# Attention output written by columns: values stationary, turned probabilities moving, reciprocal sums spread by TensorE

## What is computed

```python
# first stack, units 0 and 1: window attention with a sink; units 2 and 3: neighbourhood attention
o = jnp.einsum("bnhgqk,bnkhd->bnqhgd", p.astype(v.dtype), vw)     # window_gqa
o = jnp.einsum("brhqik,brikhd->brqhd", p, vg)                     # neighborhood_attn
y_c = window_gqa(...) * jax.nn.silu(c_z)
y_d = neighborhood_attn(...) * jax.nn.silu(d_z)
...
x + jnp.einsum("bse,ed->bsd", y, w_out)
# second stack, units 0 and 1: forgetting attention; units 2 and 3: dilated attention; no gate
```

## Time and profile before

| | |
|---|---|
| median of three runs | 1324.91 us |
| the profiled execution | 1322.76 us, span 1320.9 us |
| mean granted clock of TensorE, share of full | 0.997 |
| TensorE busy, in products / in weight loads | 1286.1 us / 1152.5 us |
| VectorE / ScalarE / GpSimd busy | 978.1 / 697.5 / 278.0 us |
| HBM read | 221.83 MB, 170 GB/s with what is written |

### The profile page before, as it was taken

How to read it: one execution, slowest core, us unless ns; L and a number is a source line. 1 busy time by engine, 2 the same in 40 slices (tenths; PEclk the granted TensorE clock), 3 DMA queues, 4 the chain that set the end, 5 groups by cost and what they waited for, 6 DMA issues and landing times.

```text
span 1320.9 us, 21359 instructions
## 1 busy us (share of the span) xinstructions
PE 1286.1 (97%) x8100; PEld 1152.5 (87%) x8100; DVE 978.1 (74%) x1172; ACT 697.5 (53%) x956; POOL 278.0 (21%) x261
## 2 busy tenths in 40 slices
PE   7999999999999999999999999999999999999997
PEld 7989998888888899988888888888889998888886
DVE  5887788788777768767877778877766867777776
ACT  5684558464444476645444445444458553644443
POOL 3755185265000024101000008200011510100000
PEclk9999999999999999999999999999999999999999
DMA  9745563457666545235766656666654424676661
GB/s 283 243 136 158 184 190 106 147 166 214 192 191 191 159 130 158 97 106 156 216 191 188 189 170 178 200 191 191 191 160 144 144 97 120 189 203 188 188 192 51
DMA packets 271551, 224.03 MB, mean 170 GB/s; under 512 B 16012, under 2 KB 254358, under 8 KB 271478
## 3 DMA queue, kind: packets, MB, share of 16 engines
q1 hardware_dynamic: 268720, 217.61, 54.9%
q0 software_dynamic: 880, 2.11, 0.9%
q10 hardware_dynamic: 1878, 3.32, 0.8%
HBM read 221.83 MB, written 3.14 MB: 170 GB/s over the span
## 4 chain that ended last, share of the span: by engine, by line
PE 85%; DVE 5%; issue 2%; ACT 2%; POOL 1%; DVEq 0%; POOLq 0%; ACTq 0%
PE wide L1620 24%; PE wide L1623 12%; PE big L1580 8%; PE big L1581 8%; PE big L1582 8%; PE wide L1580 6%; PE wide L1581 5%; PE wide L1582 5%; PE wide L1889 2%; PE wide L1740 2%; PE big L1720 1%; DVE w_lo L870 1%; PE big L1731 1%; PE big L1644 1%; DVE proj L935 1%
## 5 line engine op out<-in xcount | busy, mean ns | idle before, releaser
L870 DVE TENSOR_TENSOR w_lo<-w_raw,w_hi 128x2048 fp32r<-128x2048 f32 x203 | 472.5, 2329 | 101.7 <-ACT w_hi L455 100.8
L455 ACT ACTIVATE w_hi<-w_raw 128x2048 fp32r<-128x2048 f32 x204 | 389.9, 1911 | 198.2 <-PE big L1582 129.4
L1620 PE MATMUL wide<-h_both,w_hi 128*128 128x512 f32 x1408 | 356.7, 393 | 0.0
L1620 PEld LDWEIGHTS wide<-h_both,w_hi 128*128 128x128 f32 x1408 | 254.6, 189 | 48.6 <-DVE h_both L893 2.0
L1580 PE MATMUL wide<-h_both,w_hi 128*128 128x256 f32 x720 | 208.7, 290 | 2.6 <-DVE proj L935 2.6
L1623 PEld LDWEIGHTS wide<-h_both,w_lo 128*128 128x128 f32 x1408 | 194.2, 190 | 15.0
L1581 PE MATMUL wide<-h_both,w_hi 128*128 128x256 f32 x720 | 204.2, 284 | 0.0
L1582 PE MATMUL wide<-h_both,w_lo 128*128 128x256 f32 x720 | 204.2, 284 | 0.0
L1623 PE MATMUL wide<-h_both,w_lo 128*128 128x256 f32 x1408 | 198.8, 282 | 0.0
L1580 PE MATMUL big<-w_hi,y_hi 128*128 128x512 f32 x480 | 189.4, 395 | 0.0
L1581 PE MATMUL big<-w_lo,y_hi 128*128 128x512 f32 x480 | 187.3, 390 | 0.0
(11 more groups left out here) (246 smaller groups left out, 1529.0 us busy)
## 6 DMA issues: line engine op xcount, KB each, us to landing
w_raw<-in_w_in SPq DMA_DIRECT2D x112, 512.0 KB, 4.7
w_raw<-in_ffn_w_gate SPq DMA_DIRECT2D x88, 512.0 KB, 4.0
w_raw<-in_ffn_w_up SPq DMA_DIRECT2D x88, 512.0 KB, 5.2
w_raw<-in_ffn_w_down SPq DMA_DIRECT2D x88, 512.0 KB, 4.0
w_raw<-in_w_out SPq DMA_DIRECT2D x32, 512.0 KB, 4.3
work<-rpb_shifted SPq DMA_DIRECT2D x32, 64.0 KB, 4.2
rpb_shifted<-rpb_rows POOLq DMA_DIRECT2D x2, 735.0 KB, 7.9
pT<-in_gains ACTq DMA_DIRECT2D x2, 512.0 KB, 5.2
```

Of the source, the lines that this page charges most:

```text
L455: nc.scalar.activation(w_hi[:, r, :], w_raw[:, r, :], ACT.Copy).then_inc(hi_ready, 1)
L870: v.tensor_tensor(w_lo[:, r, :], w_raw[:, r, :], w_hi[:, r, :].bitcast(F32), ALU.subtract).then_inc(lo_ready, 1)
L1620: t_.matmul(o, hi[:, kt, c], h_both[:, kt].rearrange("p a s -> p (a s)"), start=kt == 0, stop=False, skip_group_check=True)
```

## The change

The operands of `values` change places: the values (64 columns) are stationary and the turned probabilities (128 columns) move, so `mix` comes out with the features of a head on 64 partitions and the queries along the columns, even heads in partitions 0 to 63 and odd heads in 64 to 127, two heads side by side. The output turn and `o_tm` are gone. The division must now multiply along the columns: `spread_inverse` has TensorE spread the reciprocals of a head over 64 partitions (stationary: one column of `row_inv` repeated 64 times; moving: the identity), into `aux`, for unit u - 2 in the same iteration as its `values`. In the first stack VectorE multiplies `aux` by the gate and 0.5 into `tmp` and then `mix` by `tmp`; in the second ScalarE copies `aux` to `inv_rows` (`inverse_copy`) and VectorE multiplies `mix` by it. `mix` is now freed by VectorE. `gated_y` and `plain_y` come one iteration earlier (i = 9 to 12), the pieces at i = 13 and `last_turn` are dropped, and the order of `aux` is `out9` to `out12` in place of `out10` to `out13`.

```diff
-                  if kind in ("left", "right") or (kind == "turn" and i in (7, 8)) or (kind == "out" and i >= 10)]
-               + ["cross", "ho0", "out13", "ho1", "hn0", "hn1"])
+                  if kind in ("left", "right") or (kind == "turn" and i in (7, 8)) or (kind == "out" and i >= 9)]
+               + ["cross", "ho0", "ho1", "hn0", "hn1"])
...
-        o_tm = sb("o_tm", [P, 2, NH * HD])
+        inv_rows = sb("inv_rows", [P, 2, 2 * P])
...
-            def normed_output(un, u, turned):
-
-                c = 4 * (u % 2)
-                act.wait_ge(inv_ready, un + u + 1)
-                act.wait_ge(mix_written, un + u + 2)
-                if u >= 2:
-                    act.wait_ge(aux_written, turned)
-                for s_, h in enumerate(HORDER):
-                    ins = nc.scalar.activation(o_tm[:, u % 2, h * HD:(h + 1) * HD], mix[:, h * HD:(h + 1) * HD], ACT.Copy,
-                                               scale=row_inv[:, c + s_:c + s_ + 1])
-                ins.then_inc(mix_read, 1)
+            def inverse_copy(u, written):
+
+                act.wait_ge(aux_written, written)
+                nc.scalar.activation(inv_rows[:, u % 2, :], aux[:, 0:2 * P], ACT.Copy).then_inc(aux_read, 1)
...
-                    if SC_1 + 2 <= i < SC_1 + 6:
-                        normed_output(un, i - SC_1 - 2, l * AUX_1 + i - SC_1)
...
                     if SC_2 + 2 <= i < SC_2 + 6:
-                        u = i - SC_2 - 2
-                        normed_output(un, u, ax + AUX_IX_2[f"out{i - 1}"] + 1 if u >= 2 else 0)
+                        inverse_copy(i - SC_2 - 2, ax + AUX_IX_2[f"out{i}"] + 1)
...
+                    scaled_gate = tmp[:, 0:2 * P].rearrange("p (c s) -> p c s", s=P)
                     dve.wait_ge(aux_written, n + 1)
-                    v.scalar_tensor_tensor(out=yv, in0=aux[:, 0:2 * P].rearrange("p (c s) -> p c s", s=P), scalar=0.5,
+                    v.scalar_tensor_tensor(out=scaled_gate, in0=aux[:, 0:2 * P].rearrange("p (c s) -> p c s", s=P), scalar=0.5,
                                            in1=g[:, :, cols], op0=ALU.mult, op1=ALU.mult).then_inc(aux_read, 1)
                     dve.wait_ge(aux_read, n + 2)
+                    dve.wait_ge(mix_written, un + u + 2)
+                    v.tensor_tensor(yv, mix[:, 0:2 * P].rearrange("p (c s) -> p c s", s=P), scaled_gate, ALU.mult
+                                    ).then_inc(mix_read, 1)
+                    dve.wait_ge(mix_read, un + u + 2)
...
-                        gated_y(3, 6)
-
...
-                    if 0 <= u - 3 < 3:
-                        gated_y(u - 3, 4 if u - 3 < 2 else 6)
+                    if 0 <= u - 2 < 4:
+                        gated_y(u - 2, 4 if u - 2 < 2 else 6)
...
                 def plain_y(i, kt):
-                    u = i - SC_2 - 3
-                    aux_in(f"out{i}")
+                    u = i - SC_2 - 2
+                    aux_freed(f"out{i}")
...
+                    dve.wait_ge(mix_written, un + u + 2)
+                    v.tensor_tensor(yv, mix[:, 0:2 * P].rearrange(two, s=P), inv_rows[:, u % 2, :].rearrange(two, s=P),
+                                    ALU.mult).then_inc(mix_read, 1)
+                    dve.wait_ge(mix_read, un + u + 2)
...
-                    if 0 <= u - 3 < 3:
-                        plain_y(i, 0 if u - 3 < 2 else 2)
+                    if 0 <= u - 2 < 4:
+                        plain_y(i, 0 if u - 2 < 2 else 2)
...
                 head_sums(0)
-                plain_y(NPROJ - 1, 2)
                 head_norm(0)
...
             def values(n, v_of, keys=S):
                 pe.wait_ge(pt_read, n + 2)
                 pe.wait_ge(mix_read, n + 1)
-                for s_, h in enumerate(HORDER):
+                for c in range(2):
                     for kt in range(keys // P):
-                        ins = t_.matmul(mix[:, h * HD:(h + 1) * HD], pT[:, (2 * s_ + kt) * P:(2 * s_ + kt + 1) * P],
-                                        v_of(h, kt), start=kt == 0, stop=kt == keys // P - 1, skip_group_check=True)
+                        for low in range(2):
+                            at = (2 * HORDER[2 * c + low] + kt) * P
+                            ins = t_.matmul(mix[low * HD:(low + 1) * HD, c * P:(c + 1) * P], v_of(2 * c + low, kt),
+                                            pT[:, at:at + P], start=kt == 0, stop=kt == keys // P - 1, skip_group_check=True)
                 ins.then_inc(mix_written, 1)
+
+            def spread_inverse(n, u):
+                pe.wait_ge(inv_ready, n + 1)
+                for c in range(2):
+                    for low in range(2):
+                        at = 4 * (u % 2) + HORDER[2 * c + low]
+                        ins = t_.matmul(aux[low * HD:(low + 1) * HD, c * P:(c + 1) * P],
+                                        row_inv[:, at:at + 1].to_broadcast([P, HD]), ident, start=True, stop=True,
+                                        skip_group_check=True)
+                ins.then_inc(aux_written, 1)
...
-                    if 0 <= u - 3 < 3:
+                    if 0 <= u - 2 < 4:
                         aux_free(f"out{i}")
-                        pe.wait_ge(mix_read, l * 4 + 8 + u - 3 + 2)
-                        for c in range(2):
-                            ins = t_.transpose(aux[:, c * P:(c + 1) * P], o_tm[:, (u - 3) % 2, c * P:(c + 1) * P], ident)
-                        ins.then_inc(aux_written, 1)
+                        spread_inverse(l * 4 + 8 + u - 2, u - 2)
...
-                w_out(0, {1: last_turn, 3: lambda: hgrn_out(1)})
+                w_out(0, {3: lambda: hgrn_out(1)})
```

## The result

The changed kernel takes 1322.91 us at the median (1320.66 to 1324.32, 20 runs), the kernel before on the same chip 1325.77 us (20 runs). The ratio is 0.9979, with a 95% interval of 0.9973 to 0.9985: 2.8 us or 0.21% less, 2.0 to 3.6 us by the interval. The forecast was 10.3 us less; rival (b), pairs with paid changes of tile, was 3.4 us less.

A forecast was written before the change was run, and what follows sets the result against it. TensorE, busy 97% of the span, was taken as the bound: -8.7 us of its work, -2.4 of waits that go, +0.8 of new waits, total -10.3, giving 1314.6 us. The range was 1311 to 1334, the forecast's own case 1311 to 1317.

The forecast's parts named there:

- (b): Rival: column halves run in pairs, but tile changes cost what they cost in rows, 7.7 us: 1321.5 us; 16%.
- What bounds the kernel: Whole span: TensorE, busy for 97%, sets the time; VectorE or ScalarE work counts only through TensorE's waits.
- Pairs: Values and spreads: passes in the two column halves run beside each other, 0.055 us a pass instead of 0.11.
- (c): Rival: column halves of values and spreads take turns, 8.3 us slower, 1333.2 us; 20%.
- (d): Rival: column halves take turns and changes of tile are paid, 1340.9 us or more; 7%.
- Change of tile: Entering and leaving column halves on TensorE: taken as free, between bounds of 0 and 0.14 to 0.20 us.
- the sum: TensorE's work in the attention units: values -11.8, output turns -4.2, spreads with their neighbours +7.3, together -8.7 us.
- L1963's 2.9 us: Second stack, inside w_out(0): TensorE's wait for VectorE to read a turned output goes, 1.45 us a layer.
- the give-back at the second HGRN turn: Before L1992: TensorE waits 0.8 us a layer for VectorE's L1395, leaving 0.65 a layer saved.
- The wait of L1889: TensorE's wait for VectorE to read a turned output goes, 0.6 us.
- The layer norm's: TensorE's wait before L1827, 1.2 us: 0.5 taken as saved, between nothing and all.
- The new wait before the values: First stack, iteration 10: TensorE waits for VectorE to free the values' buffer, 0.1 to 0.2 us, twice.

The follow-up runs named there:

- e2: The changed kernel with the call of `values` moved behind the scores, just ahead of the spread, in both loops: 1319.54 us, ratio 0.9956 to the kernel before.
- e1: The changed kernel with VectorE writing each reciprocal 64 times, so the spread fills the array: 1327.73 us, ratio 1.0028 to the kernel before.
- e8b: The changed kernel with the gate products of 16 stationary columns read as f32 instead of f32r: 1334.67 us in one run.
- e12: As e2, with VectorE's split of weights moved behind the second pair's sums and norm and the first gated product: 1319.90 us, ratio 0.9958.
- e3: The changed kernel with all of a unit's lower-half values passes before the upper-half ones: 1327.84 us, ratio 1.0017 to the kernel before.
- e5b: The changed kernel with a small reciprocal that VectorE then copies 64 times, so the spread fills the array: 1321.79 us, ratio 0.9969 to the kernel before.
- e7b: As e2, with VectorE summing the second pair of mixed heads before it splits a slot of weights: 1318.18 us, ratio 0.9946 to the kernel before.

## Why the prediction was wrong: its steps one by one

**What bounds the kernel: right.** TensorE is busy for 97% of the span before and after. e2 took 2.8 us of its busy time and the time fell by 3.0; e1 left its busy time low (1285.3 us) and was slower by its waits.

**Pairs: right.** Taken as 0.055 us a pass from the scores' likeness; measured 0.108 us a pair in the chain, and in the trace the records start in twos 7 ns apart (87.399, 87.406, ... 87.669, 87.676). Rivals (c) and (d), 27% together, are out. The estimate of 0.07 us a pass, from the speedup of three column tiles in the Trainium skill, page "TensorE: Matmul & The Clock Gate", section "Measured speedup vs the span model", did not hold for two f32 halves: 0.054 was measured.

**Change of tile, "I take 0": the step that failed.** It was a choice between bounds of 0 and 0.14 to 0.20, by the row thought nearest: 16-column products, "being narrow in columns as the new ones are". They were near in shape and not in type. Those rows were f32r; the new products are f32, as the scores were, and the scores were the rows with the price. Read as f32, the same 16 columns pay 0.11 and 0.20 (e8b). The sum by rival (b) was 1.92 us a layer; the chain shows its pieces at 0.14 to 0.15 into the values, out of them and into the spread, and 0.19 to 0.20 out of the spread, as priced there. The Trainium skill, page "TensorEngine Tiling (Array Packing)", section "Key Properties", says that a change of tiling mode drains the engine; the f32 halves agree, and with f32r no gap shows.

**The gain left where the sum had it.** Values fell by 12 x 0.71 + 4 x 0.25 = 9.5 us with their entries, of the 11.8 taken without; the output turns' 4.2 went. Against that stand the spreads (12 x 0.59 + 2 x 0.44 + 2 x 0.58 = 9.1, where 7.0 + 1.1 was taken) and the turns, dearer by 12 x 0.14 = 1.7, which had been put at nothing. The projection products behind a spread are dearer by 16 x 0.19, less the 0.8 spared behind scores: +2.2, where the sum had -0.8. That leaves -0.7 on TensorE where -8.7 was forecast. Of the 8.0 lost, 2.3 went at the values, 1.0 at the spreads, 1.7 at the turns and 3.0 at the projections; (b) had 7.7 in all. TensorE's busy time less the half-clock stretch gives the same -0.7.

**The waits.** L1963's 2.9 us went, as taken; the give-back at the second HGRN turn came where it was forecast, and was 1.1 us a layer instead of 0.8, so 0.35 a layer was saved and not 0.65. The wait of L1889 went in full (0.6). The layer norm's fell by 0.7 (1.2 to 0.5) where 0.5 was taken. The new wait before the values was 0.3 us, once instead of twice at 0.1 to 0.2; the stall of the last spread was 0.14, of 0.2 taken. It stayed although (b) let it go, since values and spread share a shape and no change of tile covers it.

**Size against the measurement.** The waits come to -2.9 + 2.3 - 0.6 - 0.7 + 0.3 = -1.6, with TensorE's -0.7 to -2.3; the medians show -2.8, with 0.8 us to either side. The sum from the chain and the measurement agree within that. (b), at 3.4 us less, is the rival that came true, in its mechanism too. Its chance of 16% was too low: two rows of halves with a price spoke for it, one row of another type against.

## What to carry to other kernels

A product in a part of the array costs by its neighbours too: group products of one tile shape together before counting what halves save, and count each border; it was 0.14 to 0.20 us for the f32 halves here. When a price is taken from the nearest row, the row must agree in type as well as in shape. A wait that goes by reordering can come back at the next reader of the same queue, as it did in the changed kernel and in e12: read the queue up to that reader before booking the gain.

## What the runs showed of the hardware that was not expected

- A border between tile shapes costs 0.11 to 0.20 us only where the products in part of the array are f32. As f32r, products with 16 or 64 stationary columns came and went with no gap; f32 products that fill the array follow f32r ones at once. That f32 is two records a product here may have to do with it; this wasn't tried.
- TensorE starts a pass of a free column half ahead of three that stand before it in the code: with 8 passes of one half and then 8 of the other, the first of the second 8 starts beside the fifth of the first, and a unit takes 1.51 us, not 1.90 (e3).
- VectorE's reciprocal of 128x256 takes 1.76 us and that of 128x4 0.17, where a copy of 128x256 from the same small source takes 0.29 (e1, e5b).
- A GpSimd operation of 0.20 us took 2.05 us beside VectorE's split of 128x2048 and 0.20 again with the split moved (e7b, e12). The copy of 128x256 took 0.54 and 0.58 us beside a GpSimd operation and 0.29 without one (e5b).
- Half the granted clock for 6.8 us near 76 us stands in the profiled execution of the changed kernel and not in that of before, after the same wait of 2.8 us. Both have a shorter one near 490 us. The executions of other kernels have such a stretch there or elsewhere: e2's near 77, 206 and 490 us, e7b's near 488 alone. What it turns on stays open.
